# A hybrid decoder step: which engine issues the fourth page of each group of cached keys

## The reference, cut to what matters

```
def sparse_attend(q, ks, vs, valid):
    s = jnp.einsum('bthd,btkhd->bthk', q, ks) * HEAD_DIM ** -0.5
    s = jnp.where(valid[:, :, None, :], s, -jnp.inf)
    p = jax.nn.softmax(s, axis=-1)
    return jnp.einsum('bthk,btkhd->bthd', p, vs)
# old keys of a sample: cache_k[page_table[b, j], layer, offset], a page is (128, 4 heads, 64)
```

## Time and profile before

| | |
|---|---|
| median of the three runs | 3762.4 us |
| the profiled execution's own time | 3776.25 us |
| its span | 3774.5 us |
| TensorE busy | 3324.6 us (88%) |
| VectorE busy | 1904.9 us (50%) |
| ScalarE busy | 1239.7 us (33%) |
| GpSimd busy | 646.2 us (17%) |
| transfers of `cache_k` issued by SyncE | 200, 128 KB each, 2.2 us in the median to landing |
| transfers of `cache_k` issued by ScalarE | 56, 128 KB each, 2.6 us in the median to landing |

### The profile page before, as it was taken

How to read it: one execution, slowest core, us unless ns; L and a number is a source line. 1 busy time by engine, 2 the same in 40 slices (tenths; PEclk the granted TensorE clock), 3 DMA queues, 4 the chain that set the end, 5 groups by cost and what they waited for, 6 DMA issues and landing times.

```text
span 3774.5 us, 51700 instructions
## 1 busy us (share of the span) xinstructions
PE 3324.6 (88%) x19286; PEld 2665.7 (71%) x19286; DVE 1904.9 (50%) x2988; ACT 1239.7 (33%) x2275; POOL 646.2 (17%) x651
## 2 busy tenths in 40 slices
PE   4899888867889999999868998886779999999995
PEld 2445456624889999999834544664359999999994
DVE  4569774332664434434435896733236645335335
ACT  3246713233342212212222656142342412212213
POOL 0000000001024333333100000000110334334321
PEclk8999998758999999999979999997689999999998
DMA  2111104305201111111021100232250111111111
GB/s 100 37 44 34 34 27 122 89 17 150 79 23 35 50 51 35 50 51 35 27 82 45 37 28 28 73 113 63 59 158 12 37 43 39 54 48 35 54 34 59
DMA packets 169894, 206.59 MB, mean 55 GB/s; under 512 B 61025, under 2 KB 138146, under 8 KB 168738
## 3 DMA queue, kind: packets, MB, share of 16 engines
q1 hardware_dynamic: 143138, 185.36, 16.5%
q10 hardware_dynamic: 26496, 17.84, 1.6%
HBM read 187.17 MB, written 15.96 MB: 54 GB/s over the span
## 4 chain that ended last, share of the span: by engine, by line
PE 65%; DVE 16%; ACT 8%; SPq 5%; issue 3%; DMA 2%; POOL 0%; ACTq 0%; DVEq 0%; POOLq 0%
PE PS L747 41%; PE PS L728 7%; DVE MIX L1677 4%; DVE WORK L1677 3%; PE PS L760 2%; ACT WORK L1441 2%; PE PS L832 2%; ACT X L1312 2%; DVE WORK L1865 2%; SPq L429 1%; SPq L430 1%; PE PS L940 1%; PE PS L786 1%; DMA RING<-cache_k 1%; DVE WORK L1641 1%
## 5 line engine op out<-in xcount | busy, mean ns | idle before, releaser
L747 PE MATMUL PS<-WORK_parts,WHIGH_parts 128*128 128x352 f32 x4224 | 873.1, 329 | 35.2 <-POOL WORK_parts L714 17.7
L747 PEld LDWEIGHTS PS<-WORK_parts,WHIGH_parts 128*128 128x128 f32 x4224 | 726.7, 191 | 39.0 <-issue 20.8
L728 PE MATMUL PS<-X,RING 128*128 128x512 f32 (+1 forms) x2016 | 668.6, 494 | 87.7 <-DMA RING<-w_in 66.5
L747 PE MATMUL PS<-WORK_parts,RING_parts 128*128 128x352 f32 x3168 | 693.1, 327 | 0.0
L728 PEld LDWEIGHTS PS<-X,RING 128*128 128x128 f32 x2016 | 337.2, 193 | 420.4 <-issue 350.5
L747 PEld LDWEIGHTS PS<-WORK_parts,RING_parts 128*128 128x128 f32 x3168 | 546.5, 190 | 0.0
L1677 DVE SCALAR_TENSOR_TENSOR WORK<-WORK,VEC 128x1072 f32<-128x1072 f32 (+1 forms) x236 | 477.4, 2023 | 8.4
L1258 ACT ACTIVATE WORK<-PS 128x32 f32<-128x32 f32 (+11 forms) x412 | 190.7, 514 | 826.7 <-PE PS L747 582.8
L494 POOL TENSOR_TENSOR RING_parts<-RING,WHIGH_parts 128x1024 fp32r<-128x1024 f32 (+2 forms) x184 | 372.2, 2023 | 468.9 <-ACT WHIGH_parts L1258 468.6
L747 PE MATMUL PS<-X_parts,WHIGH_parts 128*128 128x352 f32 x2016 | 435.8, 324 | 0.0
L747 PEld LDWEIGHTS PS<-X_parts,WHIGH_parts 128*128 128x128 f32 x2016 | 345.8, 189 | 0.0
(11 more groups left out here) (315 smaller groups left out, 3729.3 us busy)
## 6 DMA issues: line engine op xcount, KB each, us to landing
RING<-w_up SPq DMA_DIRECT2D x88, 512.0 KB, 3.6
RING<-cache_k SPq DMA_DIRECT2D x200, 128.0 KB, 2.2
RING<-cache_v SPq DMA_DIRECT2D x192, 128.0 KB, 2.1
RING<-w_in SPq DMA_DIRECT2D x46, 512.0 KB, 3.7
RING<-w_down SPq DMA_DIRECT2D x80, 256.0 KB, 2.7
RING<-cache_v ACTq DMA_DIRECT2D x64, 128.0 KB, 2.4
RING<-cache_k ACTq DMA_DIRECT2D x56, 128.0 KB, 2.6
yT<-X SPq DMA_DIRECT2D x5, 1408.0 KB, 5.5
```

The source lines that it names most:

```text
L728: mm = pe.matmul(job_psum(n, w, first=first), stationary(k), moving(k)[:, first:first + w], start=k == 0, stop=k == k_tiles - 1)
L747: mm = pe.matmul(thirds(n)[:, third, :], a, x[:, third * THIRD:(third + 1) * THIRD], start=k == 0 and part == 0, stop=k == tiles - 1 and p ...
```

## The change

SyncE issues all four pages of every group of keys, and ScalarE none; with the issue, ScalarE's wait for `k_used` goes too. Values stay as they were: three pages from SyncE, one from ScalarE.

```
                     elif kind in ("key", "value"):
-                        load_pages(sp, layer, name, (0, 1, 2, 3) if kind == "key" and name[1] < NSLOT else (0, 1, 2))
+                        load_pages(sp, layer, name, (0, 1, 2, 3) if kind == "key" else (0, 1, 2))
...
                         copy(FRESH[:, FRESH_TICKS.index(k), :], bank(7, NS)).then_inc(k_kept, 1)
-                    ahead = k // 2 + 2
-                    if k % 2 and NSLOT <= ahead < STREAM:
-                        act.wait_ge(k_used, ahead - NSLOT + 1)
-                        load_pages(act, layer, ("key", ahead), (3,))
```

## The result

The changed kernel took 3790.4 us (median of four runs, 3786.3 to 3797.2) against 3762.9 us before: ratio 1.0077, 95% interval [1.0061, 1.0093]. It is slower, as forecast, but the time lies 1.4 us above the range. Both kernels were run again later, with more runs: 1.0057 [1.0041, 1.0072], which is +21.5 us on a median of 3769.3 us before (29 runs, 3759.4 to 3783.2). The four runs of before in the first comparison, 3760.75 to 3764.07, lie in the lower part of that spread; whether they ran on the same chip is not on record.

What follows compares the result with a forecast made beforehand. The key-scoring stage was taken as a chain through TensorE that stops for late key pages. Longer page wait +11.5, slower clock +5 and SyncE's pace +0.5 gave +17 us on 3762.4, so 3779.4 us; range 3767 to 3789 us.

Steps and rivals of the forecast that it cites:

- Direction and cause: In key scoring, SyncE's fourth page issue becomes the last arrival in each chunk; slower, chance 0.80.
- group 4ch+3: Last key group turned in chunk ch of the scan; its load must wait until group 4ch-1 is scored.
- What goes: 56 page issues and the waits for scored keys leave ScalarE; that time alone is worth nothing on the path.
- stop before 4ch+2: TensorE's idling for ScalarE's late page 3 of that group, 20.2 us over 14 chunks; it goes, unseen in the time.
- The distance: From t0 to the first turn of group 4ch+3: from mean 5.90 to about 6.7 us per chunk, +11.5 us.
- t0: Moment in each chunk when group 4ch-1 is scored, so that loading of group 4ch+3 can start.
- TensorE's clock: One longer stop per chunk makes the work after it run at a slower clock; +5 us.
- tail: TensorE's work from the first turn of group 4ch+3 to the chunk's last scoring; 1.67 us at full clock.
- upper bound: For TensorE's clock: all 14 tails slow at 2.77 us each, +9.6 us.
- SyncE's pace: SyncE's 16 page issues per chunk are just in time, +0.5 us; as a rival setting the pace, +25 us, chance 0.12.
- The rule on issuing engines: Skill's rule by which moving a page costs next to nothing; weighed against 1.16 us per issue, 2.32 us per landing.
- The sum and its base: +17 us for the key stages, put on the three-run median 3762.4 us, giving 3779.4 us.

Runs made afterwards that it cites:

- last_page_on_act: The changed kernel, but ScalarE again issues page 3 of group 4ch+3 in each chunk; ratio 0.9998 to the kernel before.
- warm_stop: The changed kernel with 16 useless identity turns on TensorE ahead of its wait for each group 4ch+3; ratio 1.0006 to the kernel before.
- numbers_first: The changed kernel, but SyncE reads a group's four page numbers before waiting for the slot; ratio 1.0003 to the kernel before.

## Why the prediction was wrong, point by point

- *Direction and cause: right.* The fourth page on SyncE stands in the path of group 4ch+3, and giving back that one group alone returns the time (last_page_on_act). The reverse, that group alone, costs +9 us of the +21.5.
- *What goes:* right. ScalarE's freed time gave nothing, and the removed stop before 4ch+2 was not seen in the time.
- *The distance:* right. Forecast t0 + 6.7 and +11.5 us; measured 93.9 and 94.0 us in all (6.35 to 7.34 in a chunk), 11.3 to 12.1 us more than in the two profiles of before.
- *TensorE's clock: the step that failed, by its size.* The term of +5 us was 0.8 us of slowness in each tail, and nothing for the work behind a tail. Measured, with means of two profiles each: the tails are 6.9 us above before, a wholly slow one takes 2.98 us and not 2.77, the work between a tail and the next t0 is 1.7 us longer (in the second profile one stretch of 13.67 us, at granted clock 0.76, makes up all of it), and some 1 us lies at the ends of the stages (21.3 less 11.7, 6.9 and 1.7). So the term is about +9.5 us, of which 2.7 lie outside the tails. That it is the clock shows in the granted clock of these stretches, and in warm_stop, where the same wait stays and the tails run at full clock. The account of the Trainium skill that I had weighed ("TensorE: Matmul & The Clock Gate", section "HAM oscillation — how this bites in real kernels": a kernel whose DMA wait came back in every pass started each pass cold) fits most chunks and not all: 12 of the 14 tails were slowed in the first profile, 10 in the second. The tails' sum, 35.6 to 36.0 us, lies nearer to my 34.6 than to the 38.8 of the upper bound.
- *SyncE's pace:* the +0.5 us was small enough. Its waits fell to 21.0 and 20.0 us, where "some 20" was forecast. As a rival it is refuted for this kernel, where the first hand-over stands within 1 us of t0 in 25 of the 28 chunks of both profiles, and real in numbers_first.
- *The rule on issuing engines:* the Trainium skill ("DMA: Bandwidth & Descriptors", section "Issuing engines are not separate DMA queues") holds that several issuing engines save only the time to start a DMA, usually small beside the DMA itself. Only the first half agrees with these runs: issuing a page, with the reading of its number, took 1.16 us against 2.04 us for the landing in the chain above, and the fourth issue in one group per chunk cost 0.24% of the kernel alone and 0.59% with the other pages moved (1.0057 against 0.9998).
- *The sum and its base.* +17 us stands against +21.5 (15.5 to 27) in the comparison with more runs, and +29 in the first. Of the 11 us between 3779.4 and 3790.4, some 4 are the sum, nearly all of it the clock's term. The other 7 are the base, if the later median is taken for it: I put the shift on 3762.4 us, a median of three runs that agreed within 2.6 us, and took that for the kernel's spread, where 29 later runs of it span 24 us with a median of 3769.3 us. Either of the two alone would have left the time inside the range. The range was built on mechanism alone and had no room for that.

What stays open is how much of the difference between the first ratio and the second is chance and how much the chip: 29 runs of before on another chip have a median of 3765.4 us, 17 on a third 3763.9. The intervals overlap, and the traces speak for about 21 us.

## What to carry to other kernels

Where an engine's queue issues a load only when its buffer comes free, count every instruction between that moment and the last landing: the issues follow one another, and a transfer moved to that queue adds most of its issue time if its group is the one waited for (here 0.84 us of 1.16 in each chunk). Read indices ahead of the wait, so that hand-overs alone stand behind it. Price a longer stop of TensorE twice, as the wait itself and as the slow clock in the work after it. And take a kernel's spread from more than three runs before a forecast is put on their median.

## What the runs showed of the hardware that was not expected

Useless work on TensorE in a stop can be worth its weight: 16 turns in each of 14 stops of 2 to 4 us raised the granted clock of the two stages from 0.90 to 0.92 up to 0.97 and 0.98, and returned some 19 us. And the last page from SyncE for group 4ch+3, 128 KB, landed in 2.0 to 2.9 us as a rule, but took 3.2 to 3.6 us in three of 14 chunks of last_page_on_act and in five of numbers_first, for a reason that the traces do not show. It is not the change's doing: the kernel before has two such landings, of 3.46 and 3.65 us.
